# Differential-attention heads: in each excursion of TensorE the scores stand last instead of first

## The chip, the core and the metric

One core of a Trainium2 chip runs the whole program. The metric is device time in microseconds (us); three runs of the kernel before gave 782.66, 784.2 and 785.12 us, median 784.2. TensorE is called PE, VectorE DVE, ScalarE ACT, GpSimd POOL, the DMA-issuing engine SP.

## The reference

The input x is (1, 512, 1024) float32. Two layers run one after the other, each `h <- h + W_out(Mixer(RMSNorm(h)) * SiLU(z))`. The first mixer is a bidirectional state-space scan; the change does not touch it. The second is differential attention with 8 heads:

```
q, k, v, z = split(h @ w_in)                    # q, k: 8 heads x 2 maps x 64; v, z: 8 x 128
q = rmsnorm(q) * 64**-0.5 ; k = rmsnorm(k)
for each block of 128 queries:                  # 4 blocks of the 512 positions
    s    = einsum('bqhtd,bkhtd->bhtqk', q, k) + bias       # two maps t = 0, 1
    pr   = softmax(s)
    attn = pr[:, :, 0] - lam * pr[:, :, 1]
    o    = einsum('bhqk,bkhe->bqhe', attn, v)
o = rmsnorm(o) * (1 - lam_init) * silu(z) ; out = o @ w_out
```

## The kernel before

Every large product is made of three passes of matmuls (hi*hi, lo*hi, hi*lo) over operands that are split into a high and a low part. ACT writes the high part of each loaded weight tile (`w_hi`, L660), POOL subtracts it from the raw tile (`w_lo`, L503), PE multiplies (`product`, L1544).

The attention layer is software-pipelined over iterations `it` of eight stages `s`. In iteration `it` PE projects head `it` (q, k, v, z together): each stage is one `head_unit_part` of 4 row blocks x 3 passes = 12 matmuls of 128x512. Behind the projection of some stages stands an *excursion*, work of earlier heads (`stage_ops`, from L1807). With hd the head and q the query block:

- stage 1: `scores(it-2, 2)`, `o_natural(it-3)`, `probs_t(it-2, 1)`
- stage 3: `scores(it-2, 3)`, `probs_t(it-2, 2)`
- stage 4: `qk_channels(it-1)` alone
- stage 5: `scores(it-1, 0)`, `o_channels(it-3)`, `probs_t(it-2, 3)`
- stage 7: `scores(it-1, 1)`, `values(it-2)`, `probs_t(it-1, 0)`

`scores` is six matmuls with 64 rows of contraction, three into bank 4 and three into bank 5; the two maps lie in different halves of the array, so the profile merges them into three lines marked x2. `probs_t`, `o_natural` and `o_channels` are four transposes of 128x128 each, `values` is 12 matmuls into bank 7.

Each query block of a head then runs through this chain: `scores` -> DVE `biased` (adds the bias and takes the row maxima, L1332; the negated maxima are `smax`, L1336) -> ACT `exps` (two exponentials, L885) -> DVE `combine` (L1343, L1344, and `am`, L1345) -> PE `probs_t` (transposes `am`, L1773) -> ACT `probs_hi` (L892) -> DVE `probs_lo` (L1350) -> PE `values`. The output of a head goes back through the array: ACT copies bank 7 to `o_chan` (L900), PE `o_natural` (L1789), ACT squares it, DVE sums (L1382), POOL takes the power -1/2 (L494), DVE gates it into `o_nat` (L1402), PE `o_channels` (L1795).

The order of every engine is written out by hand; an engine issues in that order and waits at semaphores. What stands in a row on the other engines around the changed places:

- DVE: stage 7 `biased(it-1, 1)`, `combine(it-1, 1)`, `probs_lo(it-1, 0)`; next iteration stage 0 the sums of the squares of q and k (L1358, L1360); stage 1 `biased(., 2)`, `probs_lo(., 1)`; stage 2 the scaling of q and k (L1370, waits for POOL's power), `combine(., 2)`; stage 3 `biased(., 3)`, `probs_lo(., 2)`, the sums of the output; stage 4 `combine(., 3)`, `qT_lo` (L1392, L1395), `o_nat` (L1402); stage 5 `biased(., 0)` and so on.
- ACT: stage 7 the copies of the projection out of banks 0 to 3 (`qkvz`, L944), `exps(., 1)`, `probs_hi(., 0)`; stage 0 `w_hi`, the copy of bank 7 (L900); stage 1 `probs_hi(., 1)`, `exps(., 2)`; stage 2 `w_hi`, then `v_hi`, the gate's tanh and the squares.
- POOL: stage 0 the squares of q and k (`qk_sq`, L586), `w_lo`; stage 1 the power of 16 columns (L494); stage 2 `w_lo`, `v_lo`; stage 3 the power of 4 columns; stages 4 and 6 `w_lo`.

Iterations 0 to 3 are written out, 4 to 7 are a hardware loop of two trips with two iterations each (L1871 on). Behind it the *tail* begins, written out by hand: the output projection `out2` with the excursions of heads 6 and 7 between its parts. On POOL the tail begins with one `w_lo`, and `qk_sq` of the last head stands behind it (in the steady iterations it stands ahead).

Of the kernel before, what the change touches and what calls it, by code (L numbers as in the profile page):

```python
# [124 lines left out]
def build(nc, x, norm_w, ssd_w_in, ssd_conv_w, ssd_conv_b, ssd_dt_bias, ssd_a_log, ssd_d,  # L125
# [3 lines left out]
    with stack:  # L129
# [229 lines left out]
        def after(eng, s, n):  # L359

            if not (isinstance(n, int) and n <= 0):
                eng.wait_ge(s, n)
# [1174 lines left out]
        def _(pe):  # L1537
# [3 lines left out]
            def product(dst, a, b, first, last):  # L1541

                for n, (i, j) in enumerate(passes):
                    ins = T.matmul(dst, a[i], b[j], start=first and n == 0, stop=last and n == 2)  # L1544
                return ins
# [214 lines left out]
            def scores(hd, q):  # L1760
                pe.wait_ge(qk_lo, hd * 2 + 2)
                after(pe, smax, hd * NC + q)
                for j in range(2):
                    rs = slice(j * HD, (j + 1) * HD)
                    a = (qT_hi[rs, 0, q * P:(q + 1) * P], qT_lo[rs, 0, q * P:(q + 1) * P])
                    product(bank[4 + j][:, :], a, (qT_hi[rs, 1, :], qT_lo[rs, 1, :]), True, True)\
                        .then_inc(s_done, 1)

            def probs_t(hd, q):
                pe.wait_ge(a_done, hd * NC + q + 1)  # L1770
                after(pe, at_lo, hd * NC + q)
                for c in range(NC):
                    ins = T.transpose(bank[6][:, c * P:(c + 1) * P], am[:, q % 2, c * P:(c + 1) * P], ident[:, :])  # L1773
                ins.then_inc(t_done, 1)

            def values(hd, par_):

                pe.wait_ge(at_lo, hd * NC + NC)
                pe.wait_ge(v_lo_done, hd + 1)
                after(pe, ot_lo, hd)  # L1780
                for c in range(NC):
                    ins = product(bank[7][:, :], (v_hi[:, par_, c, :], v_lo[:, par_, c, :]),
                                  (aT_hi[:, c, :], aT_lo[:, c, :]), c == 0, c == NC - 1)
                ins.then_inc(pv_done, 1)

            def o_natural(hd):
                pe.wait_ge(o_copied, hd + 1)
                for c in range(NC):
                    ins = T.transpose(bank[7][:, c * P:(c + 1) * P], o_chan[:, c * P:(c + 1) * P], ident[:, :])  # L1789
                ins.then_inc(o_back, 1)  # L1790

            def o_channels(hd):
                pe.wait_ge(og_done, hd + 1)
                for c in range(NC):
                    ins = T.transpose(bank[7][:, c * P:(c + 1) * P], o_nat[:, c, :], ident[:, :])  # L1795
                ins.then_inc(ot_done, 1)

            def qk_channels(hd):
                pe.wait_ge(qk_ready, hd + 1)
                after(pe, smax, hd * NC)  # L1800
                for j in range(2):
                    for c in range(NC):
                        ins = T.transpose(bank[4 + j][:, c * P:(c + 1) * P],  # L1803
                                          qkvz[:, c, j * SEG:(j + 1) * SEG], ident[:, :])
                    ins.then_inc(tqk_done, 1)

            def stage_ops(m, half, s, has):  # L1807
                it = m * 2 + 2 + half
                if s == 1:
                    if has(2):  # L1810
                        scores(it - 2, 2)
                    if has(3):
                        o_natural(it - 3)
                    if has(2):
                        probs_t(it - 2, 1)
                if s == 3 and has(2):
                    scores(it - 2, 3)
                    probs_t(it - 2, 2)
                if s == 4 and has(1):
                    qk_channels(it - 1)  # L1820
                if s == 5:
                    if has(1):
                        scores(it - 1, 0)
                    if has(3):
                        o_channels(it - 3)
                    if has(2):
                        probs_t(it - 2, 3)
                if s == 7:
                    if has(1):
                        scores(it - 1, 1)  # L1830
                    if has(2):
                        values(it - 2, half)
                    if has(1):
                        probs_t(it - 1, 0)

            def out2(n, kk, rows_, done=None):

                hf, kp = O2_UNITS[n]
                u = fixed(U_O2 + n)
                k = 2 * kp + kk  # L1840
                pe.wait_ge(lo_done, u.u + 1)
                pe.wait_ge(ot_lo, k + 1)
                w = tuple(t[:, u.slot, kk * 512:kk * 512 + 512] for t in (w_hi, w_lo))
                if n == 0 and kk == 0:
                    pe.wait_ge(qkvz_in, AH * NC)
                for c in rows_:
                    if n == 3 and kk == 0:
                        pe.wait_ge(part_in, c + 1)
                    ins = product(bank[(4 if n == 6 else 0) + c][:, :], col((oT_hi, oT_lo), k, c), w,
                                  k in (0, AH - 1) or n == 6, k >= AH - 2 or (n == 2 and kk == 1))  # L1850
                if done is not None:
                    ins.then_inc(done, 1)
# [3 lines left out]
            def head_iteration(m, half, it=None):  # L1856
                def has(back):
                    return it is None or 0 <= it - back < AH
                for s in range(8):
                    if it == 0 and s == 4:  # L1860
                        pe.wait_ge(hT_lo, KT)
                    head_unit_part(head_unit(m, half, s // 2), (m * 2 + 1 + half) * NC, s // 2, s % 2)
                    if it == 0 and s == 1:
                        pe.wait_ge(h_half, 2 * NC)
                        for k in range(NC, KT):
                            next_t(k)
                    stage_ops(m, half, s, has)
# [89 lines left out]
```

## Time and profile before

| what | value |
| --- | --- |
| median of three runs | 784.2 us |
| the profiled execution: its time | 786.37 us |
| its span | 784.6 us |
| PE busy | 756.0 us (96%) |
| DVE, ACT, POOL busy | 490.5, 409.8, 454.7 us (63%, 52%, 58%) |
| granted clock of PE | 1.0 in all of the span |
| chain that ended last: share on PE | 69%, of it L1544 58% |

The span is one execution seen by the profiler. A line of a time line gives the start, the modelled duration, the engine, the line of the kernel and the tiles; in brackets stands idle time of the engine just before it and what ended it. Matmuls overlap, so what one costs on PE is the distance from its start to the next start (the *pitch*), and not its duration. In the projections the pitch is 0.23 us.

### The profile page before, as it was taken

Reading aid. Unit: us, or ns where it says so; the run is one execution under the profiler, and the core shown is the slowest. Engines: PE = TensorE matmul, PEld = TensorE weight load, DVE = VectorE, ACT = ScalarE, POOL = GpSimd, SP = SyncE. Lnnn points to the kernel's source line nnn. Section 1 sums busy time; section 2 is a strip of 40 time slices with the busy share of each in tenths; the row PEclk is TensorE's granted clock in tenths of the full one; section 3 lists DMA queues with packets and bytes.
Section 4 is the critical chain, followed back from the end, with each engine's and each line's share of the span. In section 5 each row is a group of like instructions: output and inputs, shape, how many; then the busy total and the mean of one; then the engine's idle time right before and its main releaser. Section 6 shows DMA issues by size and latency. Waiting matters only on the chain.

```text
span 784.6 us, 11675 instructions
## 1 busy us (share of the span) xinstructions
PE 756.0 (96%) x3872; PEld 612.7 (78%) x3872; DVE 490.5 (63%) x888; ACT 409.8 (52%) x818; POOL 454.7 (58%) x263
## 2 busy tenths in 40 slices
PE   6998999999999999998999999999999999999897
PEld 5777788887878788887887888777777777777676
DVE  4778957585967867595861022366667566675755
ACT  6556483828365473738541144355555555465541
POOL 6453595849476675848846335754654546545263
PEclk9999999999999999999999999999999999999999
DMA  9274464472536454552632323323223132221002
GB/s 263 57 253 108 160 162 162 109 214 66 156 128 160 161 134 160 138 186 71 194 140 88 103 85 101 108 80 92 66 81 102 54 105 58 88 88 53 1 1 108
DMA packets 100197, 91.11 MB, mean 116 GB/s; under 512 B 5456, under 2 KB 87728, under 8 KB 97080
## 3 DMA queue, kind: packets, MB, share of 16 engines
q1 hardware_dynamic: 95760, 66.99, 29.2%
q10 hardware_dynamic: 4264, 23.50, 9.7%
q8 instruction: 25, 0.41, 0.2%
q14 instruction: 20, 0.16, 0.1%
q0 software_dynamic: 128, 0.05, 0.0%
HBM read 88.13 MB, written 2.39 MB: 115 GB/s over the span
## 4 chain that ended last, share of the span: by engine, by line
PE 69%; DVE 16%; issue 6%; ACT 4%; POOL 3%; DMA 1%; DVEq 0%; POOLq 0%; ACTq 0%; SPq 0%
PE bank L1544 58%; DVE c_acc L1102 6%; PE bank L1673 2%; PE bank L1773 1%; PE bank L1647 1%; POOL w_lo L503 1%; PE bank L1659 1%; DVE tmp L1153 1%; DVE rows L1129 1%; POOL stat L494 1%; PE bank L1803 1%; ACT w_hi L660 1%; ACT c_acc L705 1%; PE bank L1621 1%; DMA rows<-in_x 1%
## 5 line engine op out<-in xcount | busy, mean ns | idle before, releaser
L503 POOL TENSOR_TENSOR w_lo<-w_raw,w_hi 128x1024 fp32r<-128x1024 f32 x104 | 257.4, 2477 | 237.4 <-ACT w_hi L660 237.1
L1544 PE MATMUL bank<-hn_hi,w_hi 128*128 128x512 f32 x384 | 154.4, 402 | 4.4 <-DVE BT L1117 3.8
L1544 PE MATMUL bank<-hn_hi,w_lo 128*128 128x512 f32 x384 | 150.1, 391 | 0.0
L1544 PE MATMUL bank<-hn_lo,w_hi 128*128 128x512 f32 x384 | 149.6, 390 | 0.0
L660 ACT CAST w_hi<-w_raw 128x1024 fp32r<-128x1024 f32 x104 | 108.2, 1044 | 69.8 <-PE bank L1544 66.0
L1544 PE MATMUL bank<-w_hi,hn_hi 128*128 128x512 f32 x320 | 128.4, 401 | 3.3 <-DVE hn_lo L1217 2.5
L1544 PE MATMUL bank<-w_hi,hn_lo 128*128 128x512 f32 x320 | 125.2, 391 | 0.0
L1544 PE MATMUL bank<-w_lo,hn_hi 128*128 128x512 f32 x320 | 124.6, 389 | 0.0
L1102 DVE SCALAR_TENSOR_TENSOR c_acc<-bank,par,c_acc 128x510 f32<-128x510 f32 (+1 forms) x128 | 95.9, 749 | 26.2 <-ACT c_acc L705 16.9
L1544 PEld LDWEIGHTS bank<-hn_hi,w_hi 128*128 128x128 f32 x384 | 72.2, 188 | 22.1 <-issue 6.5
L1544 PEld LDWEIGHTS bank<-hn_hi,w_lo 128*128 128x128 f32 x384 | 72.1, 188 | 15.7
L1544 PEld LDWEIGHTS bank<-hn_lo,w_hi 128*128 128x128 f32 x384 | 72.2, 188 | 14.2
L540 POOL TENSOR_TENSOR rows<-rows,below 128x1024 f32<-128x1024 f32 x28 | 66.7, 2400 | 22.1 <-DMA rows<-acs_rows 22.1
L1544 PEld LDWEIGHTS bank<-w_hi,hn_hi 128*128 128x128 f32 x320 | 60.1, 188 | 15.9 <-issue 4.6
L1544 PEld LDWEIGHTS bank<-w_hi,hn_lo 128*128 128x128 f32 x320 | 60.0, 188 | 13.2
L1544 PEld LDWEIGHTS bank<-w_lo,hn_hi 128*128 128x128 f32 x320 | 60.2, 188 | 11.6
L712 ACT ACTIVATE bank<-c_acc 128x512 f32<-128x512 f32 x32 | 19.3, 602 | 92.5 <-DVE c_acc L1102 92.5
L1332 DVE CUSTOM_DVE_ANT_0 sbias<-bank,wbias 128x512 f32<-128x512 f32 x64 | 41.6, 687 | 37.7 <-issue 37.7
L885 ACT ACTIVATE ex<-sbias,stat 128x512 f32<-128x512 f32 x64 | 45.8, 718 | 14.2 <-DVE stat L1336 13.9
L494 POOL TENSOR_TENSOR stat<-stat,expo 128x16 f32<-128x16 f32 (+1 forms) x16 | 31.7, 1980 | 34.9 <-DVE stat L1521 16.4
L1544 PE MATMUL bank<-w_hi,oT_hi 128*128 128x512 f32 x128 | 51.2, 400 | 0.3 <-DVE oT_lo L1463 0.3
L892 ACT CAST aT_hi<-bank 128x512 fp32r<-128x512 f32 x32 | 18.7, 584 | 60.0 <-PE bank L1773 59.7
(240 smaller groups left out, 1291.6 us busy)
## 6 DMA issues: line engine op xcount, KB each, us to landing
w_raw<-in_ssd_w_in SPq DMA_DIRECT2D x48, 512.0 KB, 4.1
w_raw<-in_attn_w_in SPq DMA_DIRECT2D x64, 256.0 KB, 3.1
rows<-acs_rows ACTq DMA_DIRECT2D x14, 1024.0 KB, 5.9
edec<-exp_rows ACTq DMA_DIRECT2D x16, 512.0 KB, 6.4
w_raw<-in_ssd_w_out SPq DMA_DIRECT2D x16, 512.0 KB, 3.7
w_raw<-in_attn_w_out SPq DMA_DIRECT2D x16, 256.0 KB, 3.1
wbias<-bias_rows SPq DMA_DIRECT2D x8, 448.0 KB, 4.4
rows<-in_x SPq DMA_DIRECT2D x4, 512.0 KB, 5.5
```

The costliest lines, as they stand in the source:

```text
L494: return nc.gpsimd.tensor_tensor(dst, src, expo[:, 0:n], ALU.pow)
L503: nc.gpsimd.tensor_tensor(w_lo[:, s, :], w_raw[:, s, :], f32(w_hi[:, s, :]), ALU.subtract)\
L540: nc.gpsimd.tensor_tensor(pair_, pair_, below[:, :, :].unsqueeze(2).to_broadcast([P, 2, NC, P]), ALU.add).then_inc(mask_done, 1)
L660: nc.scalar.copy(w_hi[:, s, :], w_raw[:, s, :]).then_inc(hi_done, 1)
L705: nc.scalar.activation(c_acc[:, p, :], b[:, :], ACT.Identity, bias=par[:, ds(t + PC_B, 1)], scale=par[:, ds(t + (PC_W + TAPS // 2 * CT), 1 ...
L712: nc.scalar.activation(bank[u.c % 2][:, :], c_acc[:, u.c % 2, :], ACT.Tanh).then_inc(tan_done, 1)
L885: nc.scalar.activation(ex[:, j, :], sbias[:, j, :], ACT.Exp, bias=stat[:, 36 + j:37 + j], accum_out=stat[:, total:total + 1]).then_inc(e_d ...
L892: nc.scalar.copy(aT_hi[:, :, q * P:(q + 1) * P], by_block(bank[6])).then_inc(at_hi, 1)
L1102: ins = V.scalar_tensor_tensor(c_acc[:, p, lo:hi], bank[p][:, lo + sh:hi + sh], par[:, ds(t + (PC_W + k * CT), 1)], c_acc[:, p, lo:hi], AL ...
L1332: ins = V.tensor_tensor_reduce(out=sbias[:, j, :], in0=bank[4 + j][:, :], in1=w, scale=1.0, scalar=-3.0e38, op0=ALU.add, op1=ALU.max, accu ...
L1544: ins = T.matmul(dst, a[i], b[j], start=first and n == 0, stop=last and n == 2)
L1673: ins = T.matmul(b[:, c * P:(c + 1) * P], prev[:, k, d, j * P:(j + 1) * P], CTr[:, c * P:(c + 1) * P], start=True, stop=True)
```

## The change

In `stage_ops` of PE the call of `scores` is moved behind the other calls of the same excursion, in stages 1, 3, 5 and 7. The excursion of stage 4 and the whole tail stay as they are, and so does the order of DVE, ACT and SP; POOL's instructions keep their order as well. The same matmuls are issued, with the same waits.

```diff
                 if s == 1:
-                    if has(2):
-                        scores(it - 2, 2)
                     if has(3):
                         o_natural(it - 3)
                     if has(2):
                         probs_t(it - 2, 1)
+                        scores(it - 2, 2)
                 if s == 3 and has(2):
+                    probs_t(it - 2, 2)
                     scores(it - 2, 3)
-                    probs_t(it - 2, 2)
                 if s == 5:
-                    if has(1):
-                        scores(it - 1, 0)
                     if has(3):
                         o_channels(it - 3)
                     if has(2):
                         probs_t(it - 2, 3)
+                    if has(1):
+                        scores(it - 1, 0)
                 if s == 7:
-                    if has(1):
-                        scores(it - 1, 1)
                     if has(2):
                         values(it - 2, half)
                     if has(1):
                         probs_t(it - 1, 0)
+                        scores(it - 1, 1)
```

PE, excursion of stage 1 in iteration 3, before (`am` is the combined map, `o_sq` the tile that holds `o_chan`, in brackets the semaphores waited for):

```order
L1544 MATMUL bank3<-w_hi,hn_lo 128x512
L1544 MATMUL bank4<-qT_hi 128x512 [waits smax,qk_lo]
L1544 MATMUL bank4<-qT_lo,qT_hi 128x512
L1544 MATMUL bank4<-qT_hi,qT_lo 128x512
L1544 MATMUL bank5<-qT_hi 128x512
L1544 MATMUL bank5<-qT_lo,qT_hi 128x512
L1544 MATMUL bank5<-qT_hi,qT_lo 128x512
L1789 MATMUL bank7<-ident,o_sq 128x128 [waits o_copied]
L1789 MATMUL bank7<-ident,o_sq 128x128 x3
L1773 MATMUL bank6<-ident,am 128x128 [waits at_lo,a_done]
L1773 MATMUL bank6<-ident,am 128x128 x3
L1544 MATMUL bank0<-w_hi,hn_hi 128x512 [waits lo_done]
```

and now:

```order
L1544 MATMUL bank3<-w_hi,hn_lo 128x512
L1789 MATMUL bank7<-ident,o_sq 128x128 [waits o_copied]
L1789 MATMUL bank7<-ident,o_sq 128x128 x3
L1773 MATMUL bank6<-ident,am 128x128 [waits at_lo,a_done]
L1773 MATMUL bank6<-ident,am 128x128 x3
L1544 MATMUL bank4<-qT_hi 128x512 [waits smax,qk_lo]
L1544 MATMUL bank4<-qT_lo,qT_hi 128x512
L1544 MATMUL bank4<-qT_hi,qT_lo 128x512
L1544 MATMUL bank5<-qT_hi 128x512
L1544 MATMUL bank5<-qT_lo,qT_hi 128x512
L1544 MATMUL bank5<-qT_hi,qT_lo 128x512
L1544 MATMUL bank0<-w_hi,hn_hi 128x512 [waits lo_done]
```

The six matmuls of the scores stand behind eight transposes instead of ahead of them; stage 3 is the same without `o_sq`.

PE, excursion of stage 5 in iteration 3, before:

```order
L1544 MATMUL bank3<-w_hi,hn_lo 128x512
L1544 MATMUL bank4<-qT_hi 128x512 [waits smax,qk_lo]
L1544 MATMUL bank4<-qT_lo,qT_hi 128x512
L1544 MATMUL bank4<-qT_hi,qT_lo 128x512
L1544 MATMUL bank5<-qT_hi 128x512
L1544 MATMUL bank5<-qT_lo,qT_hi 128x512
L1544 MATMUL bank5<-qT_hi,qT_lo 128x512
L1795 MATMUL bank7<-ident,o_nat 128x128 [waits og_done]
L1795 MATMUL bank7<-ident,o_nat 128x128 x3
L1773 MATMUL bank6<-ident,am 128x128 [waits at_lo,a_done]
L1773 MATMUL bank6<-ident,am 128x128 x3
L1544 MATMUL bank0<-w_hi,hn_hi 128x512 [waits lo_done]
```

and now:

```order
L1544 MATMUL bank3<-w_hi,hn_lo 128x512
L1795 MATMUL bank7<-ident,o_nat 128x128 [waits og_done]
L1795 MATMUL bank7<-ident,o_nat 128x128 x3
L1773 MATMUL bank6<-ident,am 128x128 [waits at_lo,a_done]
L1773 MATMUL bank6<-ident,am 128x128 x3
L1544 MATMUL bank4<-qT_hi 128x512 [waits smax,qk_lo]
L1544 MATMUL bank4<-qT_lo,qT_hi 128x512
L1544 MATMUL bank4<-qT_hi,qT_lo 128x512
L1544 MATMUL bank5<-qT_hi 128x512
L1544 MATMUL bank5<-qT_lo,qT_hi 128x512
L1544 MATMUL bank5<-qT_hi,qT_lo 128x512
L1544 MATMUL bank0<-w_hi,hn_hi 128x512 [waits lo_done]
```

The transposes that wait for the gated output (`og_done`) come straight behind the projection; the scores no longer stand between.

PE, start of the excursion of stage 7 in iteration 2, before:

```order
L1544 MATMUL bank3<-w_hi,hn_lo 128x512
L1544 MATMUL bank4<-qT_hi 128x512 [waits smax,qk_lo]
L1544 MATMUL bank4<-qT_lo,qT_hi 128x512
L1544 MATMUL bank4<-qT_hi,qT_lo 128x512
L1544 MATMUL bank5<-qT_hi 128x512
L1544 MATMUL bank5<-qT_lo,qT_hi 128x512
L1544 MATMUL bank5<-qT_hi,qT_lo 128x512
L1544 MATMUL bank7<-aT_hi,v_hi 128x512 [waits v_lo_done,at_lo]
L1544 MATMUL bank7<-aT_lo,v_hi 128x512
L1544 MATMUL bank7<-aT_hi,v_lo 128x512
```

and the end of the same excursion now:

```order
L1544 MATMUL bank7<-aT_lo,v_hi 128x512
L1544 MATMUL bank7<-aT_hi,v_lo 128x512
L1773 MATMUL bank6<-ident,am 128x128 [waits at_lo,a_done]
L1773 MATMUL bank6<-ident,am 128x128 x3
L1544 MATMUL bank4<-qT_hi 128x512 [waits smax,qk_lo]
L1544 MATMUL bank4<-qT_lo,qT_hi 128x512
L1544 MATMUL bank4<-qT_hi,qT_lo 128x512
L1544 MATMUL bank5<-qT_hi 128x512
L1544 MATMUL bank5<-qT_lo,qT_hi 128x512
L1544 MATMUL bank5<-qT_hi,qT_lo 128x512
L1544 MATMUL bank0<-w_hi,hn_hi 128x512 [waits qkvz_in,lo_done]
```

The scores stand behind twelve matmuls of the values and four transposes.

## Rows read from the trace of the kernel before

**Rows 1.** Who waited for whom, TensorE, two rows; columns: us in total, times, longest:

```profile
PE bank L1803 <- DVE stat L1336: 2.3, 1, 2.3
PE bank L1773 <- DVE am L1345: 2.2, 2, 1.8
```

**Rows 2.** Time line of TensorE, steady iteration; columns: start, us, engine, line, operation:

```profile
610.53 0.39 PE L1544 MATMUL bank<-w_hi,hn_lo 128*128 128x512 f32 x1
...
611.42 0.40 PE L1544 MATMUL bank<-qT_hi,qT_lo 64*128 64x512 f32 x2
611.75 0.50 PE L1544 MATMUL bank<-aT_hi,v_hi 128*128 128x512 f32 x1
612.09 0.40 PE L1544 MATMUL bank<-aT_lo,v_hi 128*128 128x512 f32 x1
...
614.61 0.60 PE L1773 MATMUL bank<-ident,am 128*128 128x128 f32 x4
...
615.28 0.40 PE L1544 MATMUL bank<-w_lo,hn_hi 128*128 128x512 f32 x1
...
620.32 0.39 PE L1544 MATMUL bank<-w_hi,hn_lo 128*128 128x512 f32 x1
...
627.73 0.39 PE L1544 MATMUL bank<-w_hi,hn_lo 128*128 128x512 f32 x1
...
629.68 0.39 PE L1544 MATMUL bank<-w_lo,hn_hi 128*128 128x512 f32 x1
...
635.63 0.39 PE L1544 MATMUL bank<-w_hi,hn_lo 128*128 128x512 f32 x1
```

**Rows 3.** Time line of TensorE in the tail, transposes ahead of scores:

```profile
735.06 0.60 PE L1795 MATMUL bank<-ident,o_nat 128*128 128x128 f32 x4
735.50 0.60 PE L1773 MATMUL bank<-ident,am 128*128 128x128 f32 x4
736.03 0.51 PE L1544 MATMUL bank<-qT_hi 64*128 64x512 f32 x2
...
736.60 0.41 PE L1544 MATMUL bank<-qT_hi,qT_lo 64*128 64x512 f32 x2
```

**Rows 4.** Time line of VectorE, gated output of the steady iteration:

```profile
635.00 1.12 DVE L1402 SCALAR_TENSOR_TENSOR o_nat<-bank,stat,gate 128x128 f32<-128x128 f32 x4
```

**Rows 5.** Time lines of ScalarE and GpSimd between two excursions:

```profile
613.46 0.72 ACT L885 ACTIVATE ex<-sbias,stat 128x512 f32<-128x512 f32 x1
...
615.25 0.59 ACT L892 CAST aT_hi<-bank 128x512 fp32r<-128x512 f32 x1 [0.27 <-PE bank L1773]
...
615.73 1.06 ACT L660 CAST w_hi<-w_raw 128x1024 fp32r<-128x1024 f32 x1
...
616.87 2.40 POOL L503 TENSOR_TENSOR w_lo<-w_raw,w_hi 128x1024 fp32r<-128x1024 f32 x1 [1.35 <-ACT w_hi L660]
...
619.38 2.90 POOL L494 TENSOR_TENSOR stat<-stat,expo 128x16 f32<-128x16 f32 x1
...
625.78 2.75 POOL L503 TENSOR_TENSOR w_lo<-w_raw,w_hi 128x1024 fp32r<-128x1024 f32 x1 [3.50 <-ACT w_hi L660]
```

**Rows 6.** Time lines of VectorE and GpSimd in iteration 2:

```profile
527.81 1.22 DVE L1370 TENSOR_TENSOR qkvz<-qkvz,stat 128x1024 f32<-128x1024 f32 x1 [0.93 <-POOL stat L494]
...
528.86 2.42 POOL L503 TENSOR_TENSOR w_lo<-w_raw,w_hi 128x1024 fp32r<-128x1024 f32 x1 [1.09 <-ACT w_hi L660]
...
529.45 2.39 DVE L1345 SCALAR_TENSOR_TENSOR am<-ex,stat 128x512 f32<-128x512 f32 x1
```

**Rows 7.** Time lines of GpSimd, VectorE and TensorE where the tail begins:

```profile
714.40 2.41 POOL L503 TENSOR_TENSOR w_lo<-w_raw,w_hi 128x1024 fp32r<-128x1024 f32 x1 [5.52 <-ACT w_hi L660]
...
718.70 1.22 DVE L1467 TENSOR_REDUCE stat<-qk_sq 128x16 f32<-128x1024 f32 x1 [4.29 <-POOL qk_sq L586]
...
726.23 0.75 DVE L1345 SCALAR_TENSOR_TENSOR am<-ex,stat 128x512 f32<-128x512 f32 x1
...
727.04 0.66 PE L1773 MATMUL bank<-ident,am 128*128 128x128 f32 x4 [1.84 <-DVE am L1345]
```

## Prediction

> **What bounds the kernel now.** I read the page first (PE busy for 96% of the span, the other engines 52 to 63%), then whom PE waited for, then the time lines of one steady iteration engine by engine. PE is the bound. In the attention layer its waits for VectorE are few: 2.2 us in two waits for `am`, 2.3 us in one for `smax` [rows 1]; 1.84 of the first stands in the tail [rows 7], so 0.38 is left for iteration 2, and the 2.3 is the tail's as well. In the steady iterations (3 to 7) PE waits for nobody. So the earlier transposes can't win back a wait there; the change can only alter the pitch at the joints of an excursion or bring a wait to PE that is not there now. I work both out for the steady iteration that begins at 610.53 us.
>
> **Part 1, the joints.** Start to start, before: last projection to scores to the first matmul behind them. The scores' third pair starts 0.89 us behind the last projection (610.53 to 611.42), what follows comes 0.33 later (611.75) and its second matmul 0.34 after that, where 0.23 is the pitch without a joint [rows 2]. Stage 3 takes 1.95 in all (627.73 to 629.68) [rows 2]. Now: projection to transposes 0.23, four transposes to scores 0.53 (735.50 to 736.03, the one place of the tail that has them in this order), scores to their third pair 0.57 (736.03 to 736.60) [rows 3], then 0.33 and 0.34 as above: 2.00. That is +0.05 or 0.06. Stages 1 and 5 exchange the same joints. In stage 7 the span before is 4.75 (610.53 to 615.28) [rows 2]; now 0.23, the values at 2.86 less the 0.11 of their slow first pitch (611.75 to 614.61), then 0.53, 0.57, 0.33, 0.34: 4.75, no difference. 15 excursions of the steady iterations and 3 of iterations 1 and 2 make 18 x 0.06 = **+1.1 us**. Bounds: if the 0.53 held a wait and the joint cost only 0.42 it would be -1.0, at 0.6 +2.3.
>
> **Part 2, stage 5, a wait for the gated output.** From the third pair of the scores of stage 3 (627.73 + 0.89 = 628.62) runs a chain in which nobody has slack: biased, exps, combine(3), `qT_lo`, `o_nat`. It ends at 635.00 + 1.12 = 636.12 [rows 4], 7.50 us behind that pair. PE's last projection of stage 5 is at 635.63, 7.01 behind it [rows 2]. Before, the scores stood there for 0.9 us more and hid the end of `o_nat`. Now the transposes of `o_nat` come 0.23 behind that projection, and in stage 3 no transposes stand behind the pair any more: the second projection was 1.06 behind the pair (629.68) and is now 0.33 + 0.34 = 0.67, 0.39 less. PE arrives at 7.01 - 0.39 + 0.23 = 6.85 and goes on at 7.50 + 0.06 (the 0.06 is what lay between the end of `am` and its transposes in the tail, 726.23 + 0.75 to 727.04 [rows 7]). A wait of 0.71, five times: **+3.6 us**. Bounds 0.4 and 1.0 each: 2 to 5.
>
> **Part 3, stage 7 and what it delays.** Here the scores come late: third pair at 0.23 + 2.75 + 0.53 + 0.57 = 4.08 behind the last projection instead of 0.89, +3.19. Everything that hangs on them moves: exps(1) on ScalarE, the `w_hi` behind it, on POOL `w_lo` and the power, on VectorE `combine(1)` and the scaling of q and k. Count from the third pair (C). exps starts at C + 2.04 (611.42 to 613.46). `w_hi` starts 2.27 behind that, of which the copy ahead of it stood some 0.37 for its transposes, done by then now: 1.90. `w_lo` starts 1.14 behind `w_hi`, the power 2.51 behind `w_lo` and takes 2.90 [rows 5]. The power ends at C + 10.49. The scaling follows at once (in iteration 2 VectorE waited 0.93 us for the power), `am` of block 2 starts 1.64 behind the scaling [rows 6]: C + 12.13, end C + 12.88. PE wants to transpose it in stage 3: C + 0.67 to the second projection, 620.32 - 615.28 = 5.04 to the last one, stage 1 from there 0.23 + 0.44 + 0.53 + 0.57 + 0.33 + 0.34 = 2.44 (0.44 is 735.06 to 735.50 [rows 3]), 5.04 again, and 0.23: C + 13.42. In stage 1 PE is at C + 5.94 and needs the copy of bank 7, which ScalarE ends behind `w_hi` at about C + 2.04 + 1.90 + 1.06 + 0.59 = C + 5.6; `am` of block 1 ends earlier. By this part alone nothing waits, with 0.3 to 0.5 us to spare.
>
> **Part 4, a collision on the way.** POOL's `w_lo` of stage 2 hangs on the scores of stage 1, whose third pair is now at C + 0.67 + 5.04 + 0.23 + 0.44 + 0.53 + 0.57 = C + 7.48. Before, `w_lo` started 625.78 - 620.32 - 0.89 = 4.57 behind that pair [rows 2, 5]; so it starts at C + 12.05, and `am` at C + 12.13, 0.1 us behind it. Iteration 2 shows what then happens: `w_lo` started at 528.86, `am` at 529.45, and `am` took 2.39 us instead of 0.75, to 0.56 us behind the end of `w_lo` at 531.28 [rows 6]. Where `am` is first, POOL is the one who loses: its `w_lo` at 625.78 took 2.75 us instead of 2.40 [rows 5]. With `w_lo` first, `am` ends at C + 12.05 + 2.42 + 0.56 = C + 15.03, the transposes start at C + 15.09 instead of C + 13.42: **1.7 us** a time, five times **+8.4 us**. Bounds: 0 if `am` is first each time, 8.4 if never. I take 8.4, since the sum puts `w_lo` first. In iteration 2 the collision is there already. There `w_lo` moves by 0.23 + 0.53 - 0.32 = 0.44 (the scores of iteration 1 stand behind one group of transposes), and so do `am` and its transposes, which PE waits for anyhow; and behind the transposes PE now still has the scores, 0.53 + 0.57 + 0.33 + 0.34 = 1.77 to the second projection, where it had 1.06 - 0.33 = 0.73. That is 0.44 + 1.04 less the 0.11 that the joints ahead of it brought already: **+1.4 us**.
>
> The Trainium skill, page "SBUF — State Buffer", section "Who interferes with whom", says that a VectorE instruction with two SBUF inputs and a GpSimd instruction that reads SBUF exclude each other, and whoever issues first keeps the port for the whole instruction. The rows of iteration 2 agree (2.39 us). By that rule 0.1 us of lead is enough for the full stall.
>
> **Part 5, the tail.** There `w_lo` stands ahead of `qk_sq` on POOL. `w_lo` started at 714.40, `qk_sq` right behind it, VectorE had waited 4.29 us for that and began the sums at 718.70 (714.40 + 2.41 + 1.89), and everything up to `am` of block 2, for which PE waited 1.84 us at 727.04, follows without slack [rows 7]. `w_lo` hangs on exps(1) of the last loop iteration, whose scores are 3.19 later; 0.37 of that is the copy's wait that goes. So +2.8 us on a wait that is there, and PE has no later wait that would swallow it: **+2.8 us**. Bounds 2.4 and 3.2.
>
> **Sum.** 1.1 + 3.6 + 8.4 + 1.4 + 2.8 = 17.3 us. On the profiled execution's 786.37 us that is 803.7; that execution stood 2.2 us above the median of the runs, 784.2, so the median should be **801.5 us**.
>
> **Rivals.**
> - R1, `am` is first: the 0.1 us of lead comes from eight distances of rows, each good to some hundredths, and the start of an instruction in the profile is not the moment it takes the port. Then 8.4 is away: 784.2 + 8.9 = 793.1. For it: the lead is small. Against: the nearest rows (iteration 2) have `w_lo` first and the full price.
> - R2, mixed: some of the five collide, or the stall is partial: 796 to 800.
> - R3, the steady waits don't appear (the chain to `o_nat` has slack that I don't see, as ScalarE copies the transposes earlier), and only joints, iteration 2 and the tail count: 784.2 + 5.3 = 789.5.
> - R4, faster: a joint stands behind transposes too, 0.67 from their start to the second projection (614.61 to 615.28 [rows 2]), and behind the scores. If leaving the transposes and entering the scores fell into one gap, and the one row at 0.53 held a wait for `qT_lo`, transposes to scores could be 0.35: -0.12 in 18 excursions and -0.18 in the 6 with values make -3.2, and without any wait 781.0. It decides from a pitch under 0.47 on, and only if parts 2, 4 and 5 all fail. The one row there is says 0.53, and the tail's 2.8 would have to be absent. The Trainium skill, page "TensorEngine Tiling (Array Packing)", section "Key Properties", says that a change of the tiling mode drains the engine; the 0.33 on leaving the scores, where 0.23 is the plain pitch, agrees.
>
> **Chances.** Forecast (four or five collisions) 0.5; R2 0.13; R1 0.22; R3 0.1; R4 or anything else that comes out near or under the time before 0.05. The range goes from R1 to a little over the forecast: 791.5 to 804. The forecast's own range is 799 to 804. A difference of 0.3% (2.4 us) is about what a measurement of this kernel tells from none: slower 0.95, same 0.03, faster 0.02.
>
> **What would show it.** Right: in the time line of PE the transposes L1795 of stage 5 with 0.7 us of idle time released by `o_nat` L1402, five times; the transposes L1773 of stage 3 with 1.7 us released by `am` L1345, which then lasts about 2.3 us six times instead of once; the wait at the start of the tail 4.6 us instead of 1.84; scores 0.53 behind transposes. `w_lo` of stage 2 starting a tenth ahead of `am`. Wrong: `am` at 0.75 us throughout (R1), no idle time before L1795 (R3), a pitch under 0.47 (R4).

## The result and the profile after

The changed kernel takes 804.1 us (median of 4 runs, 802.3 to 810.1) against 784.2; the ratio is 1.025 [1.021, 1.030], 19.9 us slower. The prediction said 801.5 us, range 791.5 to 804.0, slower with 0.95: the sign and the size were right and so was the place of most of the loss, and the median, 804.12, lies at the upper end of the range. The profiled execution took 803.6 us, span 801.9 us (before 786.4 and 784.6). The span difference, 17.3, equals the predicted sum, but by accident. Ahead of the attention layer this execution had 2.7 us less of a wait that the change doesn't touch (`prev` L1159, 3.4 us before). From the first transposes L1803 (506.31 before, 503.49 now) to the start of the last matmul (780.22 and 797.52) it is 273.91 and 294.03 us: +20.1, as the medians have it.

Who waited for whom, TensorE, after; columns as in [rows 1]:

```profile
PE bank L1773 <- DVE am L1345: 12.9, 7, 3.8
...
PE bank L1795 <- DVE o_nat L1402: 3.0, 5, 0.7
...
PE bank L1773 <- DVE aT_lo L1350: 1.1, 1, 1.1
PE bank L1803 <- DVE stat L1336: 1.0, 1, 1.0
...
PE bank L1544 <- DVE stat L1336: 0.8, 1, 0.8
...
PE bank L1673 <- DVE prev L1159: 0.7, 1, 0.7
```

Where [rows 1] have 2.2 us in two waits for `am`, there are seven with 12.9, and five for `o_nat` that did not exist. The lines for `aT_lo` and for L1336 ahead of the scores are new too, and the prediction has neither.

The time line of TensorE in a steady iteration, which answers to [rows 2]; columns: start, us, engine, line, operation, and in brackets the idle time before and its releaser:

```profile
601.57 0.66 PE L1773 MATMUL bank<-ident,am 128*128 128x128 f32 x4 [1.49 <-DVE am L1345]
602.15 0.50 PE L1544 MATMUL bank<-qT_hi 64*128 64x512 f32 x2
...
603.05 0.50 PE L1544 MATMUL bank<-w_hi,hn_hi 128*128 128x512 f32 x1
603.39 0.39 PE L1544 MATMUL bank<-w_lo,hn_hi 128*128 128x512 f32 x1
...
605.91 1.03 PE L1803 MATMUL bank<-ident,qkvz 128*128 128x128 f32 x8
...
609.29 0.39 PE L1544 MATMUL bank<-w_hi,hn_lo 128*128 128x512 f32 x1
610.26 0.66 PE L1795 MATMUL bank<-ident,o_nat 128*128 128x128 f32 x4 [0.58 <-DVE o_nat L1402]
610.76 0.60 PE L1773 MATMUL bank<-ident,am 128*128 128x128 f32 x4
611.29 0.51 PE L1544 MATMUL bank<-qT_hi 64*128 64x512 f32 x2
...
611.85 0.40 PE L1544 MATMUL bank<-qT_hi,qT_lo 64*128 64x512 f32 x2
612.18 0.50 PE L1544 MATMUL bank<-w_hi,hn_hi 128*128 128x512 f32 x1
...
640.93 1.03 PE L1803 MATMUL bank<-ident,qkvz 128*128 128x128 f32 x8
```

Stage 3 (601.57) waits for `am`, stage 5 (610.26) for `o_nat`, and the joints are those of Part 1: transposes to scores 0.53 (610.76 to 611.29), to the third pair 0.56, then 0.33 and 0.34. One thing about the brackets: they count from the end of the last matmul, which stands as 0.39 us long, while the next would have started 0.23 behind its start. From 609.29 to 610.26 is 0.97, so the delay is 0.74, and the idle time shows 0.58. So a stall behind a projection costs its bracket plus 0.16, and the pitch behind it is some 0.06 longer as well (0.50 for the four transposes at 610.26, where the same group without a wait takes 0.43). Read so, the period from 605.91 to 640.93 (35.02, before 32.51) holds 1.61 + 0.75 + joints.

VectorE and GpSimd ahead of stage 3 and stage 5 of the iteration behind it, and the stall on TensorE between them, which answer to [rows 4, 6]:

```profile
633.60 2.38 POOL L503 TENSOR_TENSOR w_lo<-w_raw,w_hi 128x1024 fp32r<-128x1024 f32 x1 [1.58 <-ACT w_hi L660]
...
633.79 2.73 DVE L1345 SCALAR_TENSOR_TENSOR am<-ex,stat 128x512 f32<-128x512 f32 x1
...
636.58 0.66 PE L1773 MATMUL bank<-ident,am 128*128 128x128 f32 x4 [1.45 <-DVE am L1345]
...
644.12 1.12 DVE L1402 SCALAR_TENSOR_TENSOR o_nat<-bank,stat,gate 128x128 f32<-128x128 f32 x4
...
645.29 0.66 PE L1795 MATMUL bank<-ident,o_nat 128*128 128x128 f32 x4 [0.59 <-DVE o_nat L1402]
```

`w_lo` starts 0.19 us ahead of `am`, and `am` takes 2.73 us instead of 0.75 and ends 0.54 behind `w_lo`. In the five steady iterations the lead is 0.10 to 0.30, `am` takes 2.63 to 2.82, and TensorE idles 1.59, 1.49, 1.45, 1.45 and 1.48 us. Even the lead of 0.10 brought the full price.

Iteration 2: TensorE, with the two instructions of VectorE behind its waits and the one of GpSimd beside the first of them:

```profile
516.40 1.90 POOL L586 TENSOR_TENSOR qk_sq<-qkvz 128x1024 f32<-128x1024 f32 x1 [1.52 <-ACT qkvz L944]
...
516.76 1.56 DVE L1336 TENSOR_SCALAR stat<-stat 128x2 f32<-128x2 f32 x1
...
520.48 0.39 PE L1544 MATMUL bank<-w_hi,hn_lo 128*128 128x512 f32 x1
521.92 0.63 PE L1773 MATMUL bank<-ident,am 128*128 128x128 f32 x4 [1.06 <-DVE aT_lo L1350]
...
528.44 2.36 DVE L1345 SCALAR_TENSOR_TENSOR am<-ex,stat 128x512 f32<-128x512 f32 x1
...
530.85 0.66 PE L1773 MATMUL bank<-ident,am 128*128 128x128 f32 x4 [1.74 <-DVE am L1345]
...
532.48 0.79 PE L1544 MATMUL bank<-w_hi,hn_hi 128*128 128x512 f32 x1
533.08 0.63 PE L1544 MATMUL bank<-w_lo,hn_hi 128*128 128x512 f32 x1
533.50 0.63 PE L1544 MATMUL bank<-w_hi,hn_lo 128*128 128x512 f32 x1
...
535.59 0.40 PE L1544 MATMUL bank<-w_lo,hn_hi 128*128 128x512 f32 x1
```

Two waits stand here, 1.06 us for `aT_lo` and 1.74 for `am` (0.38 before), and behind them seven matmuls at a pitch of about 0.43 instead of 0.23. Only the wait for `am` was forecast. At the top stands what the forecast left out: L1336, which takes 0.17 us where nothing is in its way, lasts 1.56 us and ends 0.02 us behind `qk_sq`. In the kernel before it had started 0.07 us ahead of `qk_sq`:

```profile
519.14 0.17 DVE L1336 TENSOR_SCALAR stat<-stat 128x2 f32<-128x2 f32 x1
...
519.21 1.90 POOL L586 TENSOR_TENSOR qk_sq<-qkvz 128x1024 f32<-128x1024 f32 x1 [1.50 <-ACT qkvz L944]
```

The tail, GpSimd, VectorE and TensorE, which answers to [rows 7]:

```profile
731.71 2.40 POOL L503 TENSOR_TENSOR w_lo<-w_raw,w_hi 128x1024 fp32r<-128x1024 f32 x1 [7.44 <-ACT w_hi L660]
734.05 1.91 POOL L586 TENSOR_TENSOR qk_sq<-qkvz 128x1024 f32<-128x1024 f32 x1
735.99 1.22 DVE L1467 TENSOR_REDUCE stat<-qk_sq 128x16 f32<-128x1024 f32 x1 [3.89 <-POOL qk_sq L586]
...
739.60 0.51 PE L1544 MATMUL bank<-qT_hi 64*128 64x512 f32 x2 [0.80 <-DVE stat L1336]
...
744.32 1.11 PE L1773 MATMUL bank<-ident,am 128*128 128x128 f32 x4 [3.75 <-DVE am L1345]
...
746.46 2.11 DVE L1336 TENSOR_SCALAR stat<-stat 128x2 f32<-128x2 f32 x1
...
748.72 1.07 PE L1803 MATMUL bank<-ident,qkvz 128*128 128x128 f32 x8 [1.05 <-DVE stat L1336]
```

The wait for `am` of block 2 is 3.75 instead of 1.84, 0.80 stands newly ahead of it, and the later wait at L1803 is 1.05 instead of 2.3.

The granted clock by stretches; columns: us, busy time and count of each engine, the granted clock (PEclk), DMA share, GB/s:

```profile
488.00:530.00 42.00, 39.19 (x183) 30.38 (x181) 22.05 (x38) 19.61 (x34) 25.98 (x11) 1.00 0.29 87
530.00:536.00 6.00, 5.15 (x19) 3.76 (x20) 2.98 (x9) 2.27 (x6) 1.93 (x2) 0.72 0.08 16
536.00:742.00 206.00, 193.34 (x962) 149.26 (x961) 127.82 (x307) 105.75 (x204) 101.84 (x46) 1.00 0.24 75
742.00:750.00 8.00, 4.63 (x20) 3.80 (x21) 7.86 (x18) 2.40 (x6) 3.35 (x3) 0.79 0.01 2
```

TensorE falls to its lower level (1.2 of 2.4 GHz) twice, behind the waits of 1.74 and 3.75 us, and in this execution nowhere in the steady iterations, whose waits are up to 1.59. Before, it stood at 1.00 in the whole layer.

From one L1803 to the next, by the same rows of both time lines:

| stretch | before | after | difference | forecast |
|---|---|---|---|---|
| first L1803 to that of iteration 2 | 28.84 | 33.26 | +4.4 | 1.5 |
| from there to that of iteration 7 (five periods) | 162.10 | 174.24 | +12.1 | 12.2 |
| from there to that of the tail | 34.16 | 37.73 | +3.6 | 3.6 |
| from there to the last matmul | 48.81 | 48.80 | 0.0 | 0 |

The forecast column is the prediction's sum put by place: five collisions (8.4), four waits for `o_nat` (2.9) and 15 joints (0.9) in the second row; the fifth wait for `o_nat` and the tail's 2.8 in the third; iteration 2 in the first.

### The profile page after: what moved, and what is told of

Same layout as the page of the kernel before. It is cut to its first block, busy times and chain, and to the rows that moved or that the text cites. A ratio compares the mean times of both kernels' runs of the same rounds, so it can differ in the third digit from the quotient of the medians.

```text
span 801.9 us, 11679 instructions
## 1 busy us (share of the span) xinstructions
PE 762.0 (95%) x3872; PEld 616.8 (77%) x3872; DVE 497.7 (62%) x888; ACT 409.7 (51%) x818; POOL 456.0 (57%) x263
## 4 chain that ended last, share of the span: by engine, by line
PE 49%; DVE 19%; issue 15%; POOL 8%; ACT 5%; DMA 1%; DVEq 1%; ACTq 0%; POOLq 0%; SPq 0%
PE bank L1544 40%; DVE c_acc L1102 6%; POOL w_lo L503 4%; POOL stat L494 2%; PE bank L1673 2%; DVE sbias L1332 2%; PE bank L1647 1%; ACT ex L885 1%; ACT w_hi L660 1%; PE bank L1659 1%; DVE tmp L1153 1%; DVE am L1345 1%; ACT c_acc L705 1%; DVE stat L1336 1%; PE bank L1621 1%
## 5 line engine op out<-in xcount | busy, mean ns | idle before, releaser
L1544 PE MATMUL bank<-w_lo,oT_hi 128*128 128x512 f32 x128 | 50.2, 393 | 0.0
```

## The experiments

All ratios are to the kernel before, timed on the same chip beside the experiment. A difference to the changed kernel is one of medians from separate series (the kernel before stood at 784.2, 785.5, 784.3 and 785.7 in the four); where it is under some 5 us the intervals overlap, and rows of the traces have to carry it. "On before" and "on after" name the kernel that was edited; lines that a diff leaves out are as in the change.

**Stage 7 alone** (on before):

```diff
                 if s == 7:
-                    if has(1):
-                        scores(it - 1, 1)
                     if has(2):
                         values(it - 2, half)
                     if has(1):
                         probs_t(it - 1, 0)
+                        scores(it - 1, 1)
```

> Scores last in stage 7 alone; stages 1, 3, 5 as before. My theory (the 1.5 us stalls of stage 3 need the late chain of stage 7 AND the scores of stage 1 behind the transposes, so that w_lo of stage 2 starts a tenth or two ahead of am): here w_lo starts 0.9 us ahead of am, am is blocked as well and lasts 2 us or less, but PE reaches its transposes only 0.2 us after am ends, so no stall of more than 0.2 us in stage 3; the tail costs 2.8 us, iteration 2 about 1: 788, +3 to +5.5 us. Rival A (the late chain alone makes the stalls): 795 or more, with five stalls at L1773. Rival B (every moved excursion costs the same, 19.9 us / 25 x 7): 789.8, with idle time in stage 7.

Measured: 789.6 us (10 runs) against 785.5, ratio 1.005 [1.002, 1.008]. `am` of block 2 is blocked in every iteration (2.4 us, `w_lo` 0.66 to 0.77 ahead), but TensorE waits only 0.29 to 0.42 for it. So the late chain alone brings the collision, and nearly all of it is hidden, as TensorE still has the scores of stage 3 ahead of the transposes. The lead was put at 0.9 and the stall at 0.2 at most; both missed a little. Rival B comes to the same time (789.8), but it asked for idle time in stage 7, and there is none. The tail has its late waits here already (0.82, 3.73 and 0.72 us), and iteration 2 a wait of 1.93.

**Stages 1, 3 and 5 alone** (the change without its last hunk):

```diff
                 if s == 3 and has(2):
+                    probs_t(it - 2, 2)
                     scores(it - 2, 3)
-                    probs_t(it - 2, 2)
...
                         probs_t(it - 2, 3)
+                    if has(1):
+                        scores(it - 1, 0)
```

> Scores last in stages 1, 3 and 5, stage 7 as before. My theory: five waits for o_nat of 0.6 us at L1795 (3 us), 17 joints of 0.06 us (1 us), no stall at the transposes of am in the steady iterations and a tail as before: 788.2, +3 to +5 us. Rival A (the stalls of stage 3 come from stages 1 and 3 themselves): +10 or more, 795. Rival B (18 of 25 equal shares of 19.9): 798.5.

Measured: 790.1 us (10), ratio 1.006 [1.003, 1.009]. The five waits for `o_nat` are there (0.67, 0.52, 0.52, 0.52, 0.53 us), `am` takes 0.75 in the steady iterations and nobody waits for it there; in iteration 2 TensorE waits 1.64 for it. With the run above: the halves cost 0.5% and 0.6%, both together 2.5%. The remaining 1.4%, 11 us, exists only where both stand; from the first L1803 to the last matmul the three traces are longer by 6.0, 6.0 and 20.1 us, which leaves 8.1.

**Stage 5 alone** (on before):

```diff
                 if s == 5:
-                    if has(1):
-                        scores(it - 1, 0)
...
                         probs_t(it - 2, 3)
+                    if has(1):
+                        scores(it - 1, 0)
```

> Scores last in stage 5 alone. My theory: PE reaches the transposes of o_nat 0.9 us earlier than before, o_nat ends 7.5 us behind the scores of stage 3 while PE is there at 7.24: five waits of 0.2 to 0.35 us, joints 0.3 us: 785.7, +1 to +2 us. Rival (o_nat had slack; its wait comes from the later scores of stage 3 only): 784.5, no wait at L1795. Rival B (equal shares, 6 of 25): 789.

Measured: 786.6 us (10), ratio 1.001 [0.997, 1.004], not told from none. The waits for `o_nat` are 0.29 once and 0.15 four times; with the 0.16 that a bracket leaves out, 0.31 a time, where Part 2 without its 0.39 of stage 3 gives 0.32. Both of its ingredients are needed: the exchange in stage 5 and the shorter way out of stage 3.

**`am` first** (on after; GpSimd holds `w_lo` of stage 2 back until `am` of block 2 is done):

```diff
                         head_norm_squares(m * 2 + 1 + half)
+                    if s == 2 and has(2):
+                        pool.wait_ge(a_done, (m * 2 + half) * NC + 3)
                     if s % 2 == 0:
```

> The changed kernel; in addition GpSimd waits in stage 2, ahead of w_lo, until am of block 2 is written, so that VectorE always goes first. If the two exclude each other and w_lo blocks am: am lasts 0.75 us everywhere in the loop, the five stalls of 1.45 to 1.6 us at L1773 go, iteration 2 loses its 1.7 and the stretch at half clock behind it (1.4 us): 794, -8 to -11 us against the changed kernel (804.1). Rival (am is late by its own chain, ScalarE's exps or the power): stalls stay, 803 to 804.

Measured: 794.1 us (5), ratio 1.013 [1.007, 1.019]: 10.0 us less than after. Time lines of VectorE and GpSimd in a steady iteration (lines are 2 higher):

```profile
626.44 2.38 POOL L503 TENSOR_TENSOR w_lo<-w_raw,w_hi 128x1024 fp32r<-128x1024 f32 x1 [2.69 <-DVE am L1347]
...
632.26 0.75 DVE L1347 SCALAR_TENSOR_TENSOR am<-ex,stat 128x512 f32<-128x512 f32 x1
...
632.67 2.59 POOL L503 TENSOR_TENSOR w_lo<-w_raw,w_hi 128x1024 fp32r<-128x1024 f32 x1
```

GpSimd waits for `am` now (first row), every `am` takes 0.75, and TensorE waits for none of them inside the loop, in iteration 2 neither, and keeps its full clock there. The same instructions run on the same engines; only who is first has changed. This is the collision's price: 7.5 + 5 x 0.16 = 8.3 in the steady iterations, 1.9 and 1.5 of slow clock in iteration 2, less 1.5 since the waits for `o_nat` grew from 3.0 to 4.5 us: 10.2 by rows, 10.0 measured. The tail is as late as before the repair (3.8 us for `am`).

**`o_nat` ahead of `qT_lo`** on VectorE (on after, stage 4; the body of either block is unchanged):

```diff
-                    if has(1):
-                        for j in range(2):
-                            dve.wait_ge(qk_hi, (it - 1) * 2 + j + 1)
...
                         ins.then_inc(og_done, 1)
+                    if has(1):
+                        for j in range(2):
+                            dve.wait_ge(qk_hi, (it - 1) * 2 + j + 1)
```

> The changed kernel; VectorE gates the output (o_nat) in stage 4 ahead of the two low parts of q and k instead of behind them. Theory: o_nat is the end of a chain that the later scores of stage 3 push out, and its two predecessors in VectorE's row take 1.3 us, more than the 0.5 to 0.7 us of each of the five waits at L1795: these go, the scores of stage 5, last in their excursion, hide the later low parts: 801, -2.5 to -3.5 us against the changed kernel (804.1). Rival (o_nat waits for the power on GpSimd or the gate, not for its turn): no change, 804; or the wait moves on to the scores, 803 to 804 with idle time before qT_hi.

Measured: 800.3 us (4), ratio 1.019 [1.012, 1.026]: 3.8 less than after, which the intervals don't tell apart. The rows do: no wait for `o_nat` is left, the five for `am` stay (1.44 to 1.58), and the five steady periods, which held four of the waits, take 171.01 us instead of 174.24, 3.2 less.

**The tail's GpSimd order** (on after): the squares of the last head ahead of `w_lo`.

```diff
-            split_lo(fixed(U_O2 + 3))
             head_norm_squares(AH - 1)
+            split_lo(fixed(U_O2 + 3))
```

> The changed kernel; in the tail GpSimd squares q and k of the last head (qk_sq) ahead of w_lo instead of behind it. Theory: the late scores of the last stage 7 reach the tail through ScalarE's w_hi, GpSimd's w_lo and qk_sq; with qk_sq ahead of w_lo VectorE's sums no longer hang on them: the waits of 0.80, 3.75 and 1.05 us that begin the tail shrink by about 3.4: 800.5, -2.5 to -4.5 us. Rival (the tail is late for its own scores or for am of block 1): 803.5 to 804.

Measured: 802.1 us (4), ratio 1.020 [1.014, 1.027], 2.0 less than after and not told from none. The waits 0.80, 3.75 and 1.05 became 1.39 and 2.33; the second is for L1336, which lasts 2.08 us behind a `w_lo`, as it did without the swap (2.11). From the L1803 of iteration 7 to that of the tail it takes 34.46 us instead of 37.73: 3.3 less, where 3.4 was expected. Behind it this execution lost 1.5 again (50.33 to the last matmul instead of 48.80), in a stretch of slow clock.

**The same order on before:**

> The kernel before with the same swap in the tail alone. Theory: the same chain was already the cause of the two waits of 1.84 and 2.33 us in the tail of before, so both go: -3.5 to -4.5 us, about 781.3 where the kernel before stands at 785.4 in this series; faster than both kernels. Rival (these waits come from the scores of head 6): no change.

Measured: 782.3 us (10), ratio 0.996 [0.992, 0.999]. The gain is 2.0, half of what was expected, and rows of VectorE, GpSimd and TensorE say why:

```profile
722.46 2.36 POOL L503 TENSOR_TENSOR w_lo<-w_raw,w_hi 128x1024 fp32r<-128x1024 f32 x1
...
722.94 1.91 DVE L1336 TENSOR_SCALAR stat<-stat 128x2 f32<-128x2 f32 x1
...
724.99 1.06 PE L1803 MATMUL bank<-ident,qkvz 128*128 128x128 f32 x8 [1.65 <-DVE stat L1336]
```

The wait for `am` is gone, but at L1803 1.65 of 2.33 us stay: L1336, 0.17 us of work on 128x2 numbers, is shut out by `w_lo` until 724.82. I had taken that wait for the length of a chain; it is a collision of the same kind, and it stood in the trace of the kernel before:

```profile
728.90 2.34 POOL L503 TENSOR_TENSOR w_lo<-w_raw,w_hi 128x1024 fp32r<-128x1024 f32 x1
...
729.18 2.08 DVE L1336 TENSOR_SCALAR stat<-stat 128x2 f32<-128x2 f32 x1
```

The Trainium skill, page "SBUF — State Buffer", section "Who interferes with whom", says that `tensor_scalar` can enter a mode in which it contends with GpSimd, and that the one that issues first keeps the ports; these rows agree (1.91 us).

**All three repairs on after:**

```diff
+                    if s == 2 and has(2):
+                        pool.wait_ge(a_done, (m * 2 + half) * NC + 3)
...
-            split_lo(fixed(U_O2 + 3))
             head_norm_squares(AH - 1)
+            split_lo(fixed(U_O2 + 3))
```

and VectorE's order of the fifth experiment.

> The changed kernel with all three repairs: GpSimd waits for am ahead of w_lo in stage 2, o_nat ahead of the low parts, qk_sq ahead of w_lo in the tail. If the three causes add up and nothing else is behind the loss, only the joints (1.1 us) and iteration 2's wait of 1.06 us are left: 794.1 - 4.4 (five waits of 0.88) - 3.5 = 786, within 2 us of the kernel before. If a further cause is hidden: 789 or more.

Measured: 787.1 us (10), ratio 1.004 [1.002, 1.007]. 17 of the 20 us are taken back with the order of TensorE untouched, though some 2 of them are the tail's swap, which shortens the kernel before as well. Of the 2.8 us that are left over the kernel before (up to 2 were expected), the rows have 1.3 up to iteration 2's L1803 (the wait for `aT_lo`), 0.4 in the five steady periods, where TensorE waits for nothing, and 1.6 behind the tail's L1803, at slow clock; the tail up to there is 0.4 shorter.

**Both collisions of the tail removed, on before:**

```diff
-            split_lo(fixed(U_O2 + 3))
             head_norm_squares(AH - 1)
+            split_lo(fixed(U_O2 + 3))
...
+            pool.wait_ge(smax, (AH - 1) * NC)
             split_lo(fixed(U_O2 + 4))
```

> The kernel before with qk_sq ahead of w_lo in the tail, and GpSimd waits for the maxima of head 6's last block (smax) before the w_lo that follows. In the run with the swap alone, 1.65 us of PE's wait for smax were left, and smax itself (L1336) lasted 1.9 us instead of 0.17 because it met that w_lo. Theory: the same exclusion as in stage 3, so smax lasts 0.17 us and the wait goes: -1.7 us more, 780.5 where the kernel before stands at 784.3. Rival (smax is late for the scores): no further change, 782.

Measured: 782.0 us (12) against 785.7 (17), ratio 0.993 [0.990, 0.996]: the fastest of all, ahead of both kernels. TensorE by stretches:

```profile
540.00:720.00 180.00, 180.00 (x905) 139.65 (x904) 115.15 (x296) 101.60 (x196) 95.44 (x44) 1.00 0.27 81
720.00:760.00 40.00, 39.69 (x209) 30.38 (x209) 27.33 (x75) 20.74 (x42) 22.55 (x13) 1.00 0.04 14
```

It is busy for 180.00 of 180 us, as it was before, and for 39.69 of 40 where the tail begins (35.53 before). Behind the first L1803 only two waits are left, 0.37 and 0.31. The gain beyond the swap itself (0.996 to 0.993) is within the intervals of the two. The rows show it: L1336 takes 0.17, the wait of 1.65 is gone, and from the L1803 of iteration 7 to that of the tail it takes 29.84 us, 31.58 with the swap alone and 34.16 before.

**Which excursion brings the stall to light** (on before: stages 1 and 7, then stages 3 and 7, each with the hunks of the change):

```diff
                         probs_t(it - 2, 1)
+                        scores(it - 2, 2)
...
                         probs_t(it - 1, 0)
+                        scores(it - 1, 1)
```

> Scores last in stages 1 and 7, stages 3 and 5 as before. By my sum w_lo of stage 2 starts 0.1 to 0.3 us ahead of am as in the full change and am ends 15.0 us behind the scores of stage 7, but PE comes to its transposes 1.0 us later since the scores of stage 3 stand ahead of them: stalls at L1773 of 0.5 to 0.8 us instead of 1.5, five times, no wait at L1795. 791. Rival (stall independent of stage 3's order): 1.5 us each, 796.

```diff
+                    probs_t(it - 2, 2)
                     scores(it - 2, 3)
-                    probs_t(it - 2, 2)
...
                         probs_t(it - 1, 0)
+                        scores(it - 1, 1)
```

> Scores last in stages 3 and 7, stages 1 and 5 as before. w_lo leads am by 0.76 us as with stage 7 alone, where the stall was 0.3 us; PE comes 0.99 us earlier to the transposes: stalls at L1773 of 1.2 to 1.4 us five times, no wait at L1795. 794. Rival (the stall needs the scores of stage 1 behind the transposes): 0.3 us each, 789.

Measured: 795.5 us (2 runs), 1.012 [1.006, 1.017], and 800.9 (2), 1.019 [1.013, 1.024]. The times lie 4.5 and 7 us above the expected ones. They carry little, with two runs each and slow clock in both tails (granted 0.87 from 720 to 760); the stalls of the steady iterations carry the argument. Idle time of TensorE ahead of `am`'s transposes, third steady iteration of each, stages 7, 1 and 7, 3 and 7:

```profile
626.95 0.66 PE L1773 MATMUL bank<-ident,am 128*128 128x128 f32 x4 [0.29 <-DVE am L1345]
```

```profile
634.63 0.66 PE L1773 MATMUL bank<-ident,am 128*128 128x128 f32 x4 [0.56 <-DVE am L1345]
```

```profile
632.06 0.66 PE L1773 MATMUL bank<-ident,am 128*128 128x128 f32 x4 [1.18 <-DVE am L1345]
```

Stage 1 adds 0.27 (its later scores bring `w_lo` and so the end of `am` later), stage 3 adds 0.89 (TensorE comes to the transposes without the scores ahead of them). 0.29 + 0.27 + 0.89 = 1.45, the stall of the full change at 636.58. The five steady periods say the same: 163.56 us with stage 7 alone, 1.8 more with stages 1 and 7, 5.5 more with 3 and 7, and 7.5 more in the full change without the waits for `o_nat` (171.01). Once `am` is shut out and its slack is used up, the shifts add.

## Why the prediction was right, step by step

- **The bound.** TensorE sets the time, and only new waits could change it. Right.
- **Part 1, joints, 1.1.** The pitches came out at 0.53, 0.56, 0.33, 0.34 against 0.53, 0.57, 0.33, 0.34, and R4 (a pitch under 0.47) is out. The sum was too large. The run with all three repairs has TensorE's new order and no wait in the five steady periods: 162.49 us against 162.10, +0.4 where 0.9 was forecast, since stage 7 gives some 0.05 back. In the full change that is made up by a term at nothing in the forecast, the longer pitch behind each of nine waits (0.6), so that the +12.1 for 12.2 owes something to luck.
- **Part 2, `o_nat`, 3.6.** Five waits of 2.96 us of idle, 3.8 with 0.16 each. Right, and shown by the run with `o_nat` early (no wait left, 3.2 us off the periods that held four of them) and by stage 5 alone (0.3 a time).
- **Part 3, stage 7.** "By this part alone nothing waits" left out that stage 7 alone already brings the collision, as `w_lo`, with the scores of stage 1 at their old place, starts even earlier. There the stall is 0.3 to 0.4. In the full change the step was right.
- **Part 4, collision, 8.4.** `w_lo` was put 0.1 ahead of `am`, it was 0.10 to 0.30; five times of five; delay 1.61 to 1.75 against 1.7; 7.5 us of idle, 8.3 with the 0.16s. Right, and shown by the run with `am` first. R1 and R2 are out, and R3 by Part 2.
- **Iteration 2, 1.4, the step that failed.** It cost 4.4 with its joints, and 1.5 was forecast. The forecast let the chain from the scores of stage 7 move by 0.44 us there. It moved by 1.8: L1336, 0.44 later than before, fell behind `qk_sq` and lasted 1.56 us instead of 0.17. Counted from the first L1803, `am` of block 2 ends at 25.53 before and at 27.31 after. In the three runs that move stage 7 and not all of the rest, L1336 lasts 1.56 as well and `am` ends at 27.28 to 27.32; with stages 1, 3 and 5 alone L1336 lasts 0.17, `am` ends at 25.92, and this stretch costs 1.5 us, as forecast. No run took this one collision away by itself. That the wait for `am` came out as forecast (1.74 for 0.38) is luck: TensorE came 1.2 us late itself, behind `aT_lo`, which hangs on the same L1336. With stages 3 and 7 the wait for `aT_lo` is 0.16, that for `am` 2.83, and the stretch just as long (33.24 us against 33.26). So the 4.4 are 1.8 for the later `am`, 1.0 for the scores that now stand behind its transposes, 1.5 of slow clock, which the forecast put at nothing, and the joint.
- **Part 5, tail, 2.8.** The difference in the table is 3.6 with the last wait for `o_nat` (0.7) in it, so 2.8 to 2.9: right. From the L1803 of iteration 7 to the end of `am` of block 2 it is 29.73 us before and 33.27 after. The tail's L1803 starts 4.43 to 4.46 us behind that end in before, in after and in every run except the one that keeps `w_lo` off L1336, where it is 2.72. So VectorE sets it, and the waits of 0.80 and 1.05 and the slow clock between them only share out that time. "PE has no later wait that would swallow it" overlooked the one at L1803, but that wait hangs on the same `am`, so it swallowed nothing.
- **The base.** Taking the 2.2 us of the profiled execution off was right for what the runs show; the 2.6 us by which the median is over 801.5 are iteration 2, which has 2.9 more than forecast in the rows.

## What to carry to other kernels

Where the bound engine never waits, reordering it can't win a wait back; look for what it pushes late on the other engines and where that lands. Check each shifted GpSimd instruction against each VectorE instruction that it now touches, the small ones too: a lead of a tenth is enough, and what the loser pays is the rest of the GpSimd instruction, so the smallest lead costs most (`am` took 2.82 us at a lead of 0.10 and 2.38 at 0.76). The repair is then a wait on GpSimd, which has time, so that the instruction TensorE hangs on is first.

## What the runs showed of the hardware

- A VectorE TENSOR_SCALAR on 128x2 f32 (0.17 us alone) took 1.56, 1.91, 2.08 and 2.11 us beside a GpSimd TENSOR_TENSOR on 128x1024 that had started first, and ended within 0.03 us of its end, while SCALAR_TENSOR_TENSOR on 128x512 ended 0.54 to 0.56 behind it.
- TensorE's granted clock went to the lower level behind waits of 1.74 and 3.75 us, and matmuls of 512 columns ran at a pitch of 0.43 instead of 0.23 us. In iteration 2 that cost 1.5 us, so a stall's price can exceed its length; in the tail it cost nothing, as TensorE had to wait for VectorE behind it. The length of one wait doesn't tell whether the clock falls: it stayed up behind 1.93 (stage 7 alone) and 1.64 us (stages 1, 3 and 5), and behind the kernel before's 1.84 and 2.33. It fell for some 7 us in the same place of the tail with waits of 1.83 and 1.90 (stage 5 alone), and once in a steady iteration right behind 1.49 us (in the run with the tail's swap on after, from 608 us on). What decides it is open.
